# ScalarE loads by name the function set that holds both the logarithm and the exponential

## The reference, cut to what matters

```python
def layer_norm(x, g, b):
    ...
    return ((xf - mu) * lax.rsqrt(var + NORM_EPS) * g.astype(jnp.float32) + b.astype(jnp.float32)).astype(x.dtype)

def rms_norm(x, g):
    ...
    return (xf * lax.rsqrt(ms + NORM_EPS) * g.astype(jnp.float32)).astype(x.dtype)

        p = jax.nn.softmax(s, axis=-1).astype(v.dtype)

    log_f = jax.nn.log_sigmoid(f_pre.astype(f32))
```

## Time and profile before

| what | value |
|---|---|
| median of 3 runs | 3022.47 us |
| the profiled execution, its own time | 3024.14 us |
| its span, first to last instruction | 3022.3 us |
| busy in the span: PE / DVE / ACT / POOL | 89% / 47% / 38% / 23% |
| ACT instructions | 1728, busy 1133.5 us |
| moved by DMA | 268.15 MB, mean 89 GB/s |

### The profile page before, as it was taken

One profiled execution on the slowest core, in us unless ns is written; L12 is line 12 of the kernel. 1 busy time (PEld: TensorE's weight loads), 2 busy tenths in 40 slices (PEclk: granted clock), 3 DMA queues, 4 the chain that ended last, 5 costly groups with the idle time before them and its releaser, 6 DMA issues.

```text
span 3022.3 us, 37518 instructions
## 1 busy us (share of the span) xinstructions
PE 2697.7 (89%) x15832; PEld 1392.7 (46%) x15832; DVE 1420.4 (47%) x2040; ACT 1133.5 (38%) x1728; POOL 689.9 (23%) x901
## 2 busy tenths in 40 slices
PE   4778998799999997799889999687788899899997
PEld 1336664355555653367534444244533334344443
DVE  3226882563331115488554422556755463243322
ACT  2556772433331114578443321332442123432222
POOL 1120000108787712100000000124333462101100
PEclk7889999899999997899989999899988899999998
DMA  6220003246552211120125532222111232233331
GB/s 224 84 84 1 2 2 120 76 155 199 191 180 98 87 60 42 47 58 2 57 83 183 185 107 85 74 77 70 56 35 42 77 105 85 69 96 100 98 101 52
DMA packets 206071, 268.15 MB, mean 89 GB/s; under 512 B 8975, under 2 KB 188558, under 8 KB 196686
## 3 DMA queue, kind: packets, MB, share of 16 engines
q1 hardware_dynamic: 199758, 243.97, 25.2%
q0 software_dynamic: 5280, 18.64, 1.8%
q10 hardware_dynamic: 864, 3.15, 0.3%
HBM read 252.62 MB, written 10.49 MB: 87 GB/s over the span
## 4 chain that ended last, share of the span: by engine, by line
PE 70%; DVE 13%; ACT 7%; POOL 3%; issue 3%; DMA 3%; SPq 0%; POOLq 0%; DVEq 0%; ACTq 0%
PE PS L285 20%; PE PS L286 19%; PE PS L287 19%; PE PS L482 2%; PE PS L846 2%; DVE SM L926 2%; DVE WB L281 2%; DVE AR L932 2%; ACT WB L271 1%; PE PS L997 1%; PE PS L1050 1%; DVE X L1095 1%; DMA WS<-in_mlp_w 1%; ACT H L1070 1%; DMA WS<-in_gqa_w_qkv 1%
## 5 line engine op out<-in xcount | busy, mean ns | idle before, releaser
L285 PE MATMUL PS<-H,WB 128*128 128x512 bf16 (+2 forms) x1896 | 696.5, 367 | 89.8 <-DVE H L1107 33.7
L281 DVE TENSOR_TENSOR WB<-WS,WB 128x2048 bf16<-128x2048 f32 (+3 forms) x165 | 370.7, 2248 | 736.1 <-ACT WB L271 735.9
L286 PE MATMUL PS<-H,WB 128*128 128x512 bf16 (+2 forms) x1896 | 695.0, 367 | 0.0
L287 PE MATMUL PS<-H,WB 128*128 128x512 bf16 (+2 forms) x1896 | 693.3, 366 | 0.0
L271 ACT ACTIVATE WB<-WS 128x2048 bf16<-128x2048 f32 (+3 forms) x165 | 295.7, 1793 | 833.8 <-PE PS L287 560.7
L285 PE MATMUL PS<-AR,WB 128*128 128x512 bf16 (+1 forms) x1172 | 419.1, 358 | 23.1 <-DVE AR L1409 9.8
L286 PE MATMUL PS<-AR,WB 128*128 128x512 bf16 (+1 forms) x1172 | 418.7, 357 | 0.0
L287 PE MATMUL PS<-AR,WB 128*128 128x512 bf16 (+1 forms) x1172 | 418.4, 357 | 0.0
L285 PEld LDWEIGHTS PS<-H,WB 128*128 128x128 bf16 (+1 forms) x1896 | 188.2, 99 | 380.7 <-issue 81.3
L287 PEld LDWEIGHTS PS<-H,WB 128*128 128x128 bf16 (+1 forms) x1896 | 190.0, 100 | 192.6 <-issue 23.7
L286 PEld LDWEIGHTS PS<-H,WB 128*128 128x128 bf16 (+1 forms) x1896 | 188.7, 100 | 176.6 <-issue 18.5
(11 more groups left out here) (381 smaller groups left out, 3759.9 us busy)
## 6 DMA issues: line engine op xcount, KB each, us to landing
WS<-in_mlp_w SPq DMA_DIRECT2D x64, 1024.0 KB, 5.5
WS<-in_w_ada SPq DMA_DIRECT2D x48, 1024.0 KB, 4.9
WS<-in_w_in SPq DMA_DIRECT2D x26, 1024.0 KB, 5.2
WS<-in_ada_w SPq DMA_DIRECT2D x24, 1024.0 KB, 5.0
WS<-in_ffn_w_in SPq DMA_DIRECT2D x44, 512.0 KB, 4.8
e_scratch<-EB POOLq DMA_DIRECT2D x16, 512.0 KB, 3.6
EB<-e_scratch POOLq DMA_DIRECT2D x16, 512.0 KB, 3.6
WS<-in_ffn_w_out SPq DMA_DIRECT2D x8, 1024.0 KB, 5.2
```

The source lines that it names most:

```text
L281: e.tensor_tensor(lo, staged(i), hi, SUB).then_inc(dv.sem, dv.mark(("lo", i)))
L285: e.matmul(out_, l[0], r[0], start=start, stop=False)
L286: e.matmul(out_, l[0], r[1], start=False, stop=False)
L287: return e.matmul(out_, l[1], r[0], start=False, stop=stop)
```

## The change

At five places the kernel calls preload_act_table_set with the set natural_log_exp_and_others, which holds both functions: at the start of ACT's program, ahead of the LN in gla_act, ahead of add_rms_act in mix_act, and ahead of rms_mod_act and of add_rms_act in ffn_act. From there on the build puts no load ahead of an LN or EXP, until a sigmoid brings another set. No computation is changed.

```diff
@@ build
+LN_EXP = "natural_log_exp_and_others"
@@ gla_act
             if i:
                 x = TM[3 + (i - 1) % 3]
+                e.preload_act_table_set(LN_EXP)
                 pe.wait_ge(e, ("ogs", i - 1))
                 e.activation(x, ps(bank_of["ogs", i - 1]), LN, bias=epsc, scale=1.0 / 128).then_inc(ac.sem, ac.mark(("free", ("ogs", i - 1))))
```

More of the change, by code:

```diff
@@ L61 @@
     wait_ge = matmul = transpose = activation = tensor_tensor = tensor_scalar = scalar_tensor_tensor = op
-    tensor_copy = memset = reciprocal = tensor_tensor_scan = copy_predicated = tensor_reduce = dma_start = op
+    tensor_copy = memset = reciprocal = tensor_tensor_scan = copy_predicated = tensor_reduce = dma_start = preload_act_table_set = op
 def rope_tables(rot, copies, pad):
```

## The result

The change takes 2977.86 us in the median (4 runs, 2977.13 to 2979.43), the kernel before beside it 3022.27 (4 runs, 3021.41 to 3028.52): a ratio of 0.9849, 95% interval 0.9832 to 0.9866, so faster by 1.5%, and the interval is far from 1. The forecast was 2972.0 with a range of 2961 to 2987: right in sign and in range, but 5.9 us too low. The profiled execution took 2979.43 us with a span of 2977.6, against a span of 3022.3 before: 44.7 us less where the sum had 50.6.

What follows compares the result with a forecast made beforehand. The chain was taken as 70% TensorE, 13% VectorE, 7% ScalarE, so only loads in it count. Terms 15.5 + 7.6 + 10.3 + 2.6 + 6.5 + 2.9 + 5.2 = 50.6 us gave 2972, range 2961 to 2987.

Steps and rivals of the forecast that it cites:

- One load, 1.29 us on the path: Anywhere in a chain of waits, a removed load saves 1.28 us plus about 0.01 of handover.
- Rival D: A load costs as much again inside neighbouring instructions: 47.7 us more, 98.3 in all, 2924; chance 0.03.
- Qkv's six waits, 15.5 us: In qkv, six TensorE waits for SQUARE with two loads ahead lose 2.58 us each.
- The clock, 7.6 us: In qkv, TensorE's clock no longer falls behind four shortened waits: 2.5, 1.7, 1.7 and 1.7 us; bounds 0 and 9.2.
- rival B: Loads go but the clock falls behind the shortened waits as well: gain 43.0 us, 2979; chance 0.18.
- wo1 and w21, 2.6 us: In these two norms the LN load is hidden while ACT waits, so only the EXP load counts: 2.6 us.
- gla_act, 2.9 us: In the mix, three EXP loads lie in the chain, the last partly hidden: 2.9 us, bounds 1.3 and 3.9.
- Last three norms, 5.2 us: EXP load of wout, both loads of ffn and EXP load of fout, 1.29 us each: 5.2 us.
- Hidden loads, nothing: Loads beside other work, such as the log-sigmoids' six, gain nothing; those six up to 0.7 us if cover goes.
- Rival C: In qkv, weight tiles take over every short wait, leaving only other stages' 27.5 us, 2995; chance 0.05.
- E: Slower: attention's 160 exponentials lengthen with the larger set; at 0.5 us more each, 3052; chance 0.02.
- F: The change doesn't do what it says, sets being switched at run time as before: 3022; chance 0.03.

Runs made afterwards that it cites:

- the fourth experiment: Changed kernel without the named load in gla_act, so its four LN and EXP pairs load their own sets again: 2980.24 us, ratio 0.9846.
- the ninth experiment: Changed kernel with eight removed loads back, each ahead of its wait, in norms wo1 and w21 and the log-sigmoids: 2977.95 us, ratio 0.9851.
- the fifth: Changed kernel with nine loads put back by name in norms wo1, w21, the mix's opening norm and the log-sigmoids: 2981.72 us, ratio 0.9859.
- the first experiment: Kernel before with only the 40 loads of the qkv stage removed, all later stages as before: 3004.37 us, ratio 0.9923.
- the third: Changed kernel with one load put back between LN and EXP in each of qkv's 20 units: 2991.57 us, ratio 0.9887.
- eighth experiments: Changed kernel with 16 idle matmuls ahead of units 4, 8 and 12 of qkv, in TensorE's long waits: 2973.93 us, ratio 0.9834.

## Why the prediction was right, and where it was off

**One load, 1.29 us on the path: right.** The short waits lost 2.6 to 2.7 us for two loads, wo1, wout and fout 1.28 or 1.29 for one. Rival D, a drain as long again, fell: it would have shown as some 2.6 us a load. The Trainium skill (ScalarE: Activation LUTs, "What ACT_TABLE_LOAD costs") states a drain of about 1380 ns beside the load; no run here shows it.

**Qkv's six waits, 15.5 us: right** (16.1 by the rows; for one, the chain has 0.37 us for the LN where it had 0.47 behind a load). The long waits stayed, and none of the short ones passed to the weight tiles.

**The clock, 7.6 us: right in three of four terms.** Behind the first three waits that had a clock gain the clock is 1.00, as forecast, worth 2.5 + 1.7 + 1.7 = 5.9 us. The term that failed is the last, 1.7 us behind the wait of 4.48: the wait became 1.91 and VectorE, not ACT, ends it, and the clock behind it is 0.68 as before. The prediction had taken it that VectorE, being earlier too, would not hold TensorE back. Besides, the rest of the stage was held fixed, and the clock behind the three long waits moved by -0.8, -0.8 and +0.6 us. The stage gave 21.7 = 16.1 by the waits and 5.6 by the clock. The time measured, 2977.9, is close to rival B's 2979, but B's reason, that the clock falls behind the shortened waits, is what happened at one of them only; the nearness is chance. The forecast's own nearness is in part chance too: the waits and the norm wo0 gave 0.6 and 0.9 us more than their terms.

**Norms wo0 and w20, 10.3 us: right** (6.0 + 4.4 measured, each within the scatter of such rows). **MLA, 6.5 us: right**, 6.4. **wo1 and w21, 2.6 us: right** for the loads, with 0.66 lost to the clock, which the sum had no term for.

**gla_act, 2.9 us: right in itself**, 2.65 in the change and 3.2 by the fourth experiment. What failed is that the mix was summed as if it ended there: three groups of eight products behind it run at 4.60 us where they had 3.51 to 4.20, and the stage keeps 1.3. The fourth experiment shows that this isn't the answer to gla_act's own loads; it comes with every version that has fewer loads in the mix, and its cause stays open.

**Last three norms, 5.2 us: off by one load.** "Both of ffn" should have been one. The LN load of ffn ran beside TensorE's last sum of squares, exactly as in wo1, where the prediction had seen it. The named loads did fit where ACT idled.

**Hidden loads, nothing: right** for the eight of the ninth experiment, and for the EXP load of the mix's norm by the fifth.

Sum of the misses against 50.6: start 1.0, qkv 1.4, w20 0.8, wo1 and w21 0.7, mix 1.6 and ffn 1.2, less 0.9 in wo0, and 0.1 in MLA: 5.9. Of these 1.2 is a load counted wrongly and 1.0 is scatter of transfers; most of the rest goes with a lower clock. Rival C fell with the first experiment; E with the unchanged 762 ns of the exponentials; F with the 73 loads gone.

What stays open is what sets the clock: waits of 2.4 us with the same work ahead went either way, and one of 1.91 us had a low clock behind it. Each run shows only the outcome.

## What to carry to other kernels

Where one engine alternates between two functions, look whether one set holds both, name it once at the start, and again behind each function that isn't in it, ahead of the wait that follows and not behind it: there a load of 1.28 us is free, behind it it is paid. Count a removed load only where nothing else was being waited for at the same time, and take the clock's gains at a discount: here 5.9 of 7.6 us came behind the shortened waits, and other stretches moved by up to 0.8 us each. Giving TensorE something to do in the long waits was worth some 4 us by itself.

## What the runs showed of the hardware that I had not expected

- The clock is not a matter of each wait alone: behind waits that the change left alone it fell for longer at two (0.72 to 0.59 over 6.0 us at the first) and for less at the third (0.50 to 0.60), and behind the stage it was low for 13.7 us in the third and eighth experiments against 6.8 in the change.
- Work whose result nobody reads can pay: 16 products of 512 columns, 3.62 us inside a wait of 4.7, and the clock behind it is 1.00 where it was 0.59.
- A load named for a set that already stands is carried out all the same: 1.28 us each in the third, fifth and ninth experiments.
- The same weight transfer took 5.05 and 6.86 us in two kernels that differ only in a stage that ends 200 us earlier.
